# The first norm's root moved behind the first layer's input products, with the rotary tables made at the first down projection

## The reference, cut to what matters

```
h = x                                        # 512 x 1024, f32
u = x * rsqrt(mean(x*x) + 1e-6) * g          # first norm, one root per token
q, k, v, glu_a, glu_g = split(u @ w_in)      # five parts of 512 columns
attn = moba_attention(q, k, v, rel_bias)     # 8 heads of 64
conv = silu(layer_norm(depthwise_conv31(glu_a * sigmoid(glu_g)) + b))
h = h + concat(attn, conv) @ w_out
h = h + (silu(norm(h) @ w_gate) * (norm(h) @ w_up)) @ w_down
h = final_norm(h)
...                                          # two more layers; the second uses
cos, sin = rope_tables(positions)            # rotary tables for its heads
```

## Time and profile before

| engine | busy us | share of span | instructions |
|---|---|---|---|
| PE | 1803.5 | 96% | 8854 |
| DVE | 1101.2 | 59% | 1640 |
| ACT | 744.2 | 40% | 1057 |
| POOL | 123.8 | 7% | 116 |

### The profile page before, as it was taken

How to read it: one execution, slowest core, us unless ns; L and a number is a source line. 1 busy time by engine, 2 the same in 40 slices (tenths; PEclk the granted TensorE clock), 3 DMA queues, 4 the chain that set the end, 5 groups by cost and what they waited for, 6 DMA issues and landing times.

```text
span 1871.9 us, 23351 instructions
## 1 busy us (share of the span) xinstructions
PE 1803.5 (96%) x8854; PEld 1450.1 (77%) x8854; DVE 1101.2 (59%) x1640; ACT 744.2 (40%) x1057; POOL 123.8 (7%) x116
## 2 busy tenths in 40 slices
PE   5997999999999999989999999999988999999998
PEld 4884788888887787768888888887855888888886
DVE  6999454444333676544767663347996367677322
ACT  4226533333323235454444452322257354454311
POOL 0100100000011111631000000100000100000000
PEclk9998999999999999989999999999999999999999
DMA  4420132232232521102322322243300223222321
GB/s 157 158 91 24 45 112 90 90 103 98 90 113 93 164 71 48 66 23 90 113 90 90 112 90 99 104 129 96 105 31 1 68 90 105 97 90 95 108 93 65
DMA packets 26407, 168.27 MB, mean 90 GB/s; under 512 B 3387, under 2 KB 3515, under 8 KB 7265
## 3 DMA queue, kind: packets, MB, share of 16 engines
q1 hardware_dynamic: 23328, 158.77, 24.7%
q0 software_dynamic: 1920, 6.42, 1.2%
q10 hardware_dynamic: 1088, 2.10, 0.5%
HBM read 163.04 MB, written 2.13 MB: 88 GB/s over the span
## 4 chain that ended last, share of the span: by engine, by line
PE 89%; DVE 7%; ACT 2%; issue 1%; DMA 0%; DVEq 0%; SPq 0%; ACTq 0%
PE ps L406 26%; PE ps L408 26%; PE ps L407 26%; PE ps L567 2%; PE ps L596 1%; PE ps L548 1%; DVE ring L1401 1%; PE ps L419 1%; PE ps L421 1%; PE ps L420 1%; ACT ring L936 1%; DVE ring L1393 1%; DVE w_lo L1159 1%; DVE score L1628 1%; PE ps L632 0%
## 5 line engine op out<-in xcount | busy, mean ns | idle before, releaser
L406 PE MATMUL ps<-a_hi,w_hi 128*128 128x512 f32 x1616 | 635.4, 393 | 9.5 <-DVE a_lo L1165 3.8
L408 PE MATMUL ps<-a_hi,w_lo 128*128 128x512 f32 x1616 | 629.8, 390 | 0.0
L407 PE MATMUL ps<-a_lo,w_hi 128*128 128x512 f32 x1616 | 629.7, 390 | 0.0
L406 PEld LDWEIGHTS ps<-a_hi,w_hi 128*128 128x128 f32 x1616 | 303.9, 188 | 84.9 <-issue 16.3
L408 PEld LDWEIGHTS ps<-a_hi,w_lo 128*128 128x128 f32 x1616 | 303.8, 188 | 63.7
L407 PEld LDWEIGHTS ps<-a_lo,w_hi 128*128 128x128 f32 x1616 | 304.0, 188 | 63.4 <-issue 1.4
L1159 DVE TENSOR_TENSOR w_lo<-raw,w_hi 128x2048 fp32r<-128x2048 f32 x82 | 192.2, 2344 | 227.0 <-ACT w_hi L789 227.0
L789 ACT CAST w_hi<-raw 128x2048 fp32r<-128x2048 f32 x82 | 156.0, 1903 | 315.4 <-PE ps L408 275.5
L406 PE MATMUL ps<-h_hi,w_hi 128*128 128x512 f32 x528 | 206.2, 391 | 0.0
L408 PE MATMUL ps<-h_hi,w_lo 128*128 128x512 f32 x528 | 205.4, 389 | 0.0
L407 PE MATMUL ps<-h_lo,w_hi 128*128 128x512 f32 x528 | 205.4, 389 | 0.0
(11 more groups left out here) (227 smaller groups left out, 1972.6 us busy)
## 6 DMA issues: line engine op xcount, KB each, us to landing
raw<-weights_dram SPq DMA_DIRECT2D x148, 1024.0 KB, 4.8
bias_t<-bias_rows_scratch POOLq DMA_DIRECT2D x8, 256.0 KB, 4.8
ncb<-decay_rows_scratch POOLq DMA_DIRECT2D x8, 256.0 KB, 5.7
out_dram<-xT SPq DMA_DIRECT2D x8, 256.0 KB, 2.0
xT<-x_in_dram ACTq DMA_DIRECT2D x4, 256.0 KB, 6.2
xT<-x_in_dram SPq DMA_DIRECT2D x4, 256.0 KB, 9.1
ring<-qk ACTq DMA_DIRECT2D x32, 32.0 KB
v<-pT POOLq DMA_DIRECT2D x1, 1016.0 KB, 6.7
```

Source lines behind the costliest of these rows:

```text
L406: pe.matmul(dst, wh, hi[:, k0 + k, :], start=start and k == 0, stop=False)
L407: pe.matmul(dst, wh, lo[:, k0 + k, :], start=False, stop=False)
L408: last = pe.matmul(dst, wl, hi[:, k0 + k, :], start=False, stop=stop and k == nk - 1)
```

## The change

Six edits go together.

1. DMAs at the start: SP loads the gains alone, then slab 0 in three parts (512, 512 and 1024 columns) between the odd chunks of x, then slab 1, the squares, and the rest of the vectors. ACT issues the even chunks. POOL no longer loads the positions here.
2. `a_hi` and `a_lo` are made from x times gain without the root, chunk by chunk as x lands (`first_high`, `low_x`); slab 0 is split in three parts. PE starts slab 0 on these.
3. Squares and their sum are interleaved behind that work; PE's sum over features comes inside slab 1, ahead of its third chunk.
4. The root is multiplied in behind the products. Slabs 0 to 3: DVE multiplies the gate from PSUM by the root (`glu_r`), ACT takes the sigmoid, POOL multiplies the sigmoid by the root (`scaled_gate`), DVE multiplies value by that. q and k: POOL multiplies each pair in `qk1` (`qk_r`). v: PE transposes the root to one number per token after slab 2, DVE copies it to `small`, and ACT applies it as the scale of four copies of 256 columns in place of one of 1024.
5. The rotary tables move to the start of `late_down("down1")` on DVE and ACT; POOL loads the positions after its products with the root.
6. The taps are dealt out anew: 97 in the loop over slabs (was 101), 27 beside the attention (was 23): two at each of units 0 to 10, was 0 to 6.

```
--- SP
+sp.dma_start(vec[:, 0:gains], vectors[:, 0:gains]).then_inc(sem["gain_in"], 16)
+sp.dma_start(raw[:, 0, 0:512], weights[0][:, 0:512]).then_inc(sem["w0_in"], 16)
+sp.dma_start(xT[:, 1, :], x_in[1]).then_inc(s_x[1], 16)
+sp.dma_start(raw[:, 0, 512:1024], weights[0][:, 512:1024]).then_inc(sem["w0_in2"], 16)
+sp.dma_start(xT[:, 3, :], x_in[3]).then_inc(s_x[3], 16)
+sp.dma_start(raw[:, 0, 1024:2048], weights[0][:, 1024:2048]).then_inc(landed[0], 16)
+for c in (5, 7): sp.dma_start(xT[:, c, :], x_in[c]).then_inc(s_x[c], 16)
+sp.dma_start(raw[:, 1, :], weights[1]).then_inc(landed[1], 16)
 sp.dma_start(sq_f[:, :, :], squares[:, :, :]).then_inc(sem["consts"], 16)
+sp.dma_start(vec[:, gains:NCOL], vectors[:, gains:NCOL]).then_inc(sem["consts"], 16)
--- POOL
+def scaled_gate(j):
+    wait("glu_g", j + 1)
+    if j: wait("glu", j)
+    nc.gpsimd.tensor_tensor(tmp[:, 2, :], tmp[:, 0, :], tmp[:, 5, :], ALU.mult).then_inc(sem["glu_s"], 1)
+scaled_gate(0)
 ...                                   # bias rows out to DRAM and back, as before
+for j in range(1, 4): scaled_gate(j)
+for j in range(4):
+    wait("qkv", j + 1)
+    nc.gpsimd.tensor_tensor(pair, pair, rows, ALU.mult).then_inc(sem["qk_r"], 1)
+pool.dma_start(sinT[:, :].bitcast(I32), positions.to_broadcast([P, S])).then_inc(sem["turns_in"], 16)
--- PE
-pe.wait_ge(sem["consts"], 32)
-wait("add0", DC - 1)
-pe.matmul(ps[:, BT, :], ones, tmp[:, 3, :], start=True, stop=True).then_inc(sem["sums"], 1)
+feature_major(0, ..., a_hi, a_lo, 0, DC, True, True, first_chunks).then_inc(sem["slab"], 1)
 for j in range(10):
+    if j: project("in1", j, first_sum if j == 1 else None, tokens=j >= 8)   # the sum at chunk 2
+    if j == 2:
+        wait("rstd", 1)
+        for t in range(QT): m = pe.transpose(ps[:, BT + 1, ...], tmp[:, 5, ...], ident)
+        m.then_inc(sem["rtok0_mm"], 1)
 ...                                   # attention: scores of units 0 and 1 also
+wait("qk_r", 4)
--- ACT
+A.copy(w_hi[:, 0, 0:512], raw[:, 0, 0:512]); first_high(0); first_high(1)
+A.copy(w_hi[:, 0, 512:1024], ...); first_high(2); squares_of(0, 0)
+A.copy(w_hi[:, 0, 1024:2048], ...)
+for c in range(3, DC):
+    first_high(c); squares_of(0, c - 2)
+split(1); squares_of(0, 6); squares_of(0, 7)
 root(0)
+act.preload_act_table_set("sigmoid_and_others")
 for j in range(10):
     if j < 4:
+        wait("glu_r", j + 1)
+        if j: wait("glu_s", j)
+        A.activation(tmp[:, 0, :], tmp[:, 1, :], ACT.Sigmoid).then_inc(sem["glu_g"], 1)
     split(n + 2)
 ...                                   # v: four copies with a scale per token
+for t in range(QT): last = A.activation(to, part, ACT.Copy, scale=small[:, 8 + t:9 + t])
--- DVE
+first_split(0, 512, 1); low_x("norm0", 0, 0); low_x("norm0", 0, 1)
+first_split(512, 1024, 2); low_x("norm0", 0, 2)
+first_split(1024, 2048, 3)
+for c in range(3, DC):
+    low_x("norm0", 0, c)
+    if c > 3: first_add(c - 3)
+first_add(5); split(1); first_add(6); first_add(7)
 for j in range(10):
     if j < 4:
+        wait("slab", BASE["in1"] + j + 1)
+        if j == 0: wait("rstd", 1)
+        Vv.tensor_tensor(tmp[:, 1, :], ps[:, gate bank, :], tmp[:, 5, :], ALU.mult).then_inc(sem["glu_r"], 1)
+    if j: taps(3)                      # j == 0: the two copies of the bias rows
     split(BASE["in1"] + j + 2)
     if j < 4:
+        wait("glu_s", j + 1)
+        Vv.tensor_tensor(cu[:, j, PADL:PADL + S], ps[:, value bank, :], tmp[:, 2, :], ALU.mult)
+    taps(4 if j == 0 else 7 if j < 4 else 9)
 ...                                   # beside(i)
-taps(2 if i < 7 else 1)
+taps(2 if i < 11 else 1)
--- late_down("down1") on DVE and on ACT, at its head
+turns()        # DVE: 7 operations of 512 columns; ACT: Sin, Abs, Sin, then the table set of before
```

More of the change, by code:

```diff
@@ L335, in _ @@
                 pool.dma_start(bias_t[:, h, :], mirrored).then_inc(sem["bias_out"], 16)
+            for j in range(1, 4):
+                scaled_gate(j)
+            rows = tmp[:, 5, :].unsqueeze(1).to_broadcast([P, 2, S])
+            for j in range(4):
+                wait("qkv", j + 1)
+                pair = qk1[:, 2 * j:2 * j + 2, :]
+                nc.gpsimd.tensor_tensor(pair, pair, rows, ALU.mult).then_inc(sem["qk_r"], 1)
+            pool.dma_start(sinT[:, :].bitcast(I32), positions.to_broadcast([P, S])).then_inc(sem["turns_in"], 16)
             def add_squares(k):
@@ L809, in root, with first_high, turns @@
                 A.activation(tmp[:, 5, :], tmp[:, 4, :], ACT.Exp, scale=-0.5).then_inc(sem["rstd"], 1)
[L811 to L815, removed]
+            def first_high(c):
+                act.wait_ge(s_x[c], 16)
+                A.activation(a_hi[:, c, :], xT[:, c, :], ACT.Copy, scale=col("gain", c)).then_inc(sem["ahi"], 1)
+            def turns():
+                wait("rope_dve", 6)
+                A.activation(sinT[:, :], cosT[:, :], ACT.Sin, scale=col("rot_sign")).then_inc(sem["rope_act"], 1)
+                A.activation(tmp[:, 1, :], cosT[:, :], ACT.Abs).then_inc(sem["rope_act"], 1)
+                wait("rope_act", 2)
+                A.activation(cosT[:, :], tmp[:, 1, :], ACT.Sin, bias=col("half_pi"), scale=-1.0
+                             ).then_inc(sem["rope_act"], 1)
             def out_phase(name, k):
@@ L1017, in attend @@
                         A.copy(a_hi[:, 4 + u.p, :], qk2[:, 8 + u.p, :]).then_inc(sem["ahi"], 1)
-            for c in range(1, DC, 2):
+            for c in range(0, DC, 2):
                 act.dma_start(xT[:, c, :], x_in[c]).then_inc(s_x[c], 16)
             act.preload_act_table_set("natural_log_exp_and_others")
-            for c in range(DC):
-                squares_of(0, c)
+            wait("w0_in", 16)
+            A.copy(w_hi[:, 0, 0:512], raw[:, 0, 0:512]).then_inc(sem["w0_hi"], 1)
+            wait("gain_in", 16)
+            first_high(0)
+            first_high(1)
+            wait("w0_in2", 16)
+            A.copy(w_hi[:, 0, 512:1024], raw[:, 0, 512:1024]).then_inc(sem["w0_hi"], 1)
+            first_high(2)
+            squares_of(0, 0)
+            act.wait_ge(landed[0], 16)
+            A.copy(w_hi[:, 0, 1024:2048], raw[:, 0, 1024:2048]).then_inc(sem["whi"], 1)
+            for c in range(3, DC):
+                first_high(c)
+                squares_of(0, c - 2)
+            split(1)
+            squares_of(0, 6)
+            squares_of(0, 7)
             act.wait_ge(sem["consts"], 32)
-            split(0)
             root(0)
[L1028 to L1035, removed]
+            act.preload_act_table_set("sigmoid_and_others")
             for j in range(10):
@@ L1040, in _ @@
                 if j < 4:
[L1041 to L1046, removed]
+                    wait("glu_r", j + 1)
+                    if j:
+                        wait("glu_s", j)
+                    A.activation(tmp[:, 0, :], tmp[:, 1, :], ACT.Sigmoid).then_inc(sem["glu_g"], 1)
                 if j < 9:
@@ L1055, in _ @@
                     else:
-                        A.copy(v1[:, :, 256 * (j - 8):256 * (j - 7)], bank.rearrange(
-                            "p b (t c) -> p (b t) c", c=256)).then_inc(sem["qkv"], 1)
+                        wait("rtok0", 1)
+                        for t in range(QT):
+                            to, part = v1[:, t, 256 * (j - 8):256 * (j - 7)], bank[:, t // 2, t % 2 * 256:t % 2 * 256 + 256]
+                            last = A.activation(to, part, ACT.Copy, scale=small[:, 8 + t:9 + t])
+                        last.then_inc(sem["qkv"], 1)
             act.preload_act_table_set("natural_log_exp_and_others")
@@ L1166, in low, with first_split @@
                                  ).then_inc(sem["alo"], 1)
[L1168 to L1180, removed]
+            def first_split(lo, hi, part):
+                wait("w0_hi" if part < 3 else "whi", part if part < 3 else 1)
+                Vv.tensor_tensor(w_lo[:, 0, lo:hi], raw[:, 0, lo:hi], w_hi[:, 0, lo:hi].bitcast(F32), ALU.subtract
+                                 ).then_inc(sem["w0_lo" if part < 3 else "wlo"], 1)
@@ L1231, in late_down @@
             def late_down(name, norm, k):
+                if k == 2:
+                    turns()
                 for p in range(4):
@@ L1467, in attend @@
                         low(4 + u.p, qk2[:, 8 + u.p, :], FILL[name] + fills[name])
[L1469 to L1474, removed]
+            first_split(0, 512, 1)
+            dve.wait_ge(sem["gain_in"], 16)
+            low_x("norm0", 0, 0)
+            low_x("norm0", 0, 1)
+            first_split(512, 1024, 2)
+            low_x("norm0", 0, 2)
+            first_split(1024, 2048, 3)
+            for c in range(3, DC):
+                low_x("norm0", 0, c)
+                if c > 3:
+                    first_add(c - 3)
+            first_add(5)
+            split(1)
+            first_add(6)
+            first_add(7)
             dve.wait_ge(sem["consts"], 32)
-            dve.wait_ge(sem["pos_in"], 32)
+            dve.wait_ge(sem["pos_in"], 16)
```

(5 more changed lines are left out.)

81 lines of the change are left out of this document (65 added, 16 removed).

## The result

The kernel after takes 1876.59 us (median of 20 runs), the kernel before 1873.72 (20 runs): a ratio of 1.0015, 95% interval 1.0009 to 1.0022. The interval excludes 1: with 20 runs each, 0.15% can be told from nothing, where the prediction put the limit at 0.2%. The forecast was 1866.3, so 10.3 us are missing. The profiled execution of after took 1876.53, with a span of 1874.7 against 1871.9.

A forecast was written before the change was run, and what follows sets the result against it. PE was taken to bound nearly everywhere, DVE the first attention. 10.3 earlier at the projection's end, less 0.5 (DVE), 0.3 (v) and 2.0 (taps), gave 7.5 less: 1866.3 us, own range 1863.5 to 1869.5, outer 1862.5 to 1871.8.

The forecast's parts named there:

- Does DVE keep pace?: First projection's slabs: DVE beside POOL's gate and q, k products loses 0.5 us, between 0 and 14.2.
- The prediction's own sign: First projection: the forecast is wrong on POOL if taps lengthen by more than a tenth; expected hardly longer than 0.74.
- The third rival: First projection: POOL's products stop DVE for 14.2 us, 1.1 taken by a gap; 1878.9 us, chance 0.08.
- point of decision: First projection: DVE loss from which POOL's products stopping DVE decides, 9.1 us, 64% of POOL's time.
- the 0.25 and 0.4: Earlier trace's splits beside POOL's additions: 2.54 for 2.29, longest 2.70; taken as DVE losing 0 to 0.4 a meeting.
- a shorter form of that rule: POOL beside DVE: skill's key point that GpSimd contends with DVE instructions that have two SBUF inputs; no size given.
- Start: First layer: PE starts slab 0 near 7.1, slab 1 at 24.8 in place of 36.87, gaining 12.1 us.
- Sum, transposes: Added to PE in the first projection: sum over features inside slab 1, 1.0 us; four transposes after slab 2, 0.6.
- End of the projection: First projection ends 10.3 us earlier: 12.1 less 1.0, 0.6 and a 0.2 stall, if DVE keeps pace.
- v: First attention: four copies of 256 columns in place of one cost 0.3 us, between 0 and 0.7.
- The attention's taps: First attention: four more taps, at units 7 to 10, cost 2.0 us, between 0.7 and 2.7.
- The tables: First down projection: moved tables delay ACT's first cast from 489.9 to 493.0, hidden from PE with 3.6 us to spare.

The follow-up runs named there:

- the second experiment: Kernel after with POOL's q, k and gate products all cut to one column, DVE multiplying value by the bare sigmoid: 1866.66 us, ratio 0.9963.
- the first experiment: Kernel after with POOL's products of q and k cut to one column of each chunk, gate products whole: 1866.51 us, ratio 0.9959 to the kernel before.

## Why the prediction was wrong

The step that failed is **Does DVE keep pace?**, its conclusion that DVE loses "0 to 0.4 in a meeting and POOL the rest" and the value of 0.5. Measured, DVE lost 1.0 in each of three gate products and 2.1 in each of four products of q and k, 11.4 in sum, and of these the 8.5 of q and k arrived at the attention. The prediction's own sign came as well: the 120 taps lengthened by more than a tenth, to a mean of 838 ns against 740 to 757 before. The third rival names the mechanism that came. Its price was too high (14.2, all but 1.1 of it on the path) by the shorter hold, 2.1 for a pair and 1.0 for a gate. Its point of decision, 9.1, lies between the 8.5 of q and k and the 11.4 in sum. The gates' 3.0 cost nothing once q and k are free (the second experiment); in the kernel after, where the chain runs over their taps too, how much of the 3.0 counts is open, since no run takes out the gates alone.

What misled me are the earlier trace rows. They show a split of DVE alone beside a run of POOL's additions, and there POOL paid. I carried the 0.25 over to rows of twelve taps without a gap, of which no row of before showed one beside POOL, and which paid 2.1. But the 0.25 and 0.4 were no price of a meeting. One of the two longest kinds of split in before, and the additions of POOL beside it:

```profile
241.39 2.83 POOL L343 TENSOR_TENSOR tmp<-tmp 128x512 f32<-128x512 f32 x2 [9.44 <-ACT tmp L802]
```

```profile
243.66 2.70 DVE L1159 TENSOR_TENSOR w_lo<-raw,w_hi 128x2048 fp32r<-128x2048 f32 x1 [2.04 <-ACT w_hi L789]
```

The second addition runs to 244.22, 0.56 past the start of the split, and the split is 0.42 longer than its 2.28. So it is with all 14 splits of before that took over 2.36: each began while an addition was running, and its excess is what was left of that addition, less about 0.13. The taps of after follow the same count, less 0.20: the one at 73.92 takes 2.0 more, and the product had 2.2 left, to 76.14. A split that meets only the end of an addition pays little; in a row without gaps the next tap begins early in the product's run and pays nearly all of it. The trace of before thus already agreed with the third rival, and I read what was left of an addition as a price.

The other sign was that the stretch had next to no slack: at 10.86 of 10.90 busy on DVE, with one idle stretch of 1.26 at its end, a term between 0 and 14.2 had to be weighed as the largest in the sum, and I took its lower end.

The Trainium skill (SBUF — State Buffer, Who interferes with whom) says that a DVE instruction with two SBUF inputs contends with a GpSimd instruction that reads SBUF, and that one with at most one SBUF input, outside DVE's modes that use two ports, does not; it calls the shared pair of ports an exclusive lock. The runs agree in both halves: 2887 ns with two, 752 and 756 with one. In the prediction I let count against a shorter form of that rule.

The other steps, by the first experiment, which is the change without the disputed products (1866.51 against the 1866.3 forecast):

- *Start.* PE's first matmul near 7.1 forecast, 8.85 measured in the kernel after, which costs nothing, since slab 0 and the bias rows end before slab 1's low part. Slab 1 at 24.8 forecast, 25.03 measured. Sum, transposes: 1.02 and 0.60 as taken. End of the projection 10.3 earlier forecast; PE takes the first scores 10.07 earlier (126.21 against 136.28). Right.
- *v.* 1.57 for four copies against 1.01: 0.56 where I took 0.3, inside the bound of 0.7.
- *The attention's taps.* 2.0 taken. In the first experiment, as in before, the first units wait for ACT's table load; from its end (129.2, before 138.7) to the first matmul of the out projection (179.02, before 186.94) the attention grew by 1.6. In the kernel after nothing waits for the load, and it grew by 1.2 from DVE's first scores. Too high, inside its bounds of 0.7 and 2.7.
- *The tables.* In the kernel after, ACT's first cast of the first down projection starts at 494.23 against 489.90, 3.3 later against its slab; PE doesn't wait there. Right.
- *Later layers.* I had no term there. Between 205 us and the end the profiled executions drift against that of before, although q, k and the taps lie behind them: by +1.8 (after), +2.0 (root by DVE), +0.8 (no products of q and k), +0.5 (products in the kernel before), +0.4 (taps from PSUM), -1.4 (sums in PSUM), -1.5 (no product at all). Nearly all of it comes in the second and the third attention, as in the kernel after. The windows above show the clock's lower level no longer around the first step than in before, so the cause stays open; no run here tests it.

Of the profiled execution's +2.8, then, 1.0 stands at the end of the first attention and 1.8 is this drift. That the first experiment comes so close to the forecast is partly luck: 10.1 less 0.56 and 1.6 is 7.9, the drift of 0.8 takes it to 7.2, and the forecast had 7.5 by 10.3 less 0.5, 0.3 and 2.0.

## What to carry to other kernels

An idle engine's time is free only if its work doesn't hold the engine that paces the stretch: before moving work to GpSimd, list the VectorE instructions beside it, and where those with both inputs in SBUF follow one another without a gap, count nearly the full length of each GpSimd operation as lost to VectorE (here 2.1 of 2.40 and 1.0 of 1.29). If VectorE has to stay there, put one of its operands in PSUM (here four sums of 128 x 512 f32, in four free banks) before moving the work back: here that was worth 10 us (1876.59 to 1866.38). Where a trace has only single meetings, set the excess against the end of the operation that was met: what is left of that operation is no price for a row without gaps.

## What the runs showed of the hardware

- A GpSimd product with SBUF operands and a VectorE instruction with two SBUF inputs exclude each other: one tap of a row takes up to 2.89 us in place of 0.75, 2.1 more, for a product that takes 2.40 beside taps with one input in PSUM.
- A split or tap that begins beside a running GpSimd operation is longer by what is left of that operation, less about 0.13 (splits) or 0.20 (taps): so in the 14 of before and the 21 of after that are lengthened. An operation that is itself still held lengthens none.
- It isn't always VectorE that waits. Behind a row without gaps a product of 2 x 128 elements lasted 5.59, 4.86 and 4.15 (the first experiment), one of 1024 columns 10.45 and 10.47. Each got through where the next split of VectorE ended: the small ones were done 0.05 behind that, the large ones 2.3. Why a split lets a product in and most taps don't, I didn't find.
- A tap costs the same with its sum in PSUM (median 744 ns, read and written there) as in SBUF (746).
